# A router that reads the output projection's transposed result, with x kept transposed

## What is computed

```python
h = jnp.einsum('btd,de->bte', x, w_in)                 # 2048 -> 4352
...                                                    # conv, chunk MLP, pooling give y (2048 wide)
mix = jnp.einsum('bte,ed->btd', y, w_out)              # 2048 -> 2048
x = layer_norm(ALPHA * x + mix, ln1_g, ln1_b)
g_logits = (xt @ rg_w).astype(jnp.float32) + rg_b      # 4 expert groups, top 1
e_logits = ((xt @ re_w).astype(jnp.float32) + re_b)    # 16 experts, top 2 within the group
hg = jnp.einsum('nd,edf->nef', xt, w_gate)             # 2048 -> 512 for each of 16 experts
hu = jnp.einsum('nd,edf->nef', xt, w_up)
a = jax.nn.silu(hg) * hu * combine[:, :, None]
out = jnp.einsum('nef,efd->nd', a, w_down)
x = layer_norm(ALPHA * x + out, ln2_g, ln2_b)
```

## Time and profile before

| | us |
|---|---|
| median of 3 runs (lowest, highest) | 895.5 (894.67, 897.81) |
| the profiled execution, its own time | 897.55 |
| its span | 895.7 |
| PE busy | 838.7 |
| DVE, ACT, POOL busy | 282.4, 263.8, 24.8 |
| mixer, to the last chunk's end | about 0 to 394 |
| router, to the first expert matmul | about 394 to 427 |
| experts and the last LayerNorm | about 427 to 896 |

### The profile page before, as it was taken

One profiled execution on the slowest core, in us unless ns is written; L12 is line 12 of the kernel. 1 busy time (PEld: TensorE's weight loads), 2 busy tenths in 40 slices (PEclk: granted clock), 3 DMA queues, 4 the chain that ended last, 5 costly groups with the idle time before them and its releaser, 6 DMA issues.

```text
span 895.7 us, 11202 instructions
## 1 busy us (share of the span) xinstructions
PE 838.7 (94%) x4729; PEld 558.7 (62%) x4729; DVE 282.4 (32%) x390; ACT 263.8 (29%) x465; POOL 24.8 (3%) x41
## 2 busy tenths in 40 slices
PE   6999999999999999995989999999999998897993
PEld 6989999999999999983433334433333333333331
DVE  6273384434764435355000102043003220022203
ACT  5234232322233323312432332432223322133101
POOL 0000000000001000001000000000000100000000
PEclk8999999999999999996899999999999999999997
DMA  9643553665444774459898999999999999999980
GB/s 298 185 142 120 188 164 127 192 205 164 144 140 153 282 282 141 141 220 384 353 426 351 421 423 422 428 418 423 424 425 420 424 426 420 422 424 425 421 355 37
DMA packets 81149, 267.80 MB, mean 299 GB/s; under 512 B 5626, under 2 KB 58320, under 8 KB 59657
## 3 DMA queue, kind: packets, MB, share of 16 engines
q1 hardware_dynamic: 78042, 258.92, 74.6%
q0 software_dynamic: 1984, 5.31, 1.5%
q10 hardware_dynamic: 1078, 2.94, 1.0%
HBM read 263.07 MB, written 11.54 MB: 307 GB/s over the span
## 4 chain that ended last, share of the span: by engine, by line
PE 68%; DMA 18%; DVE 6%; ACT 3%; SPq 2%; issue 2%; POOL 0%; POOLq 0%; ACTq 0%; DVEq 0%
PE ps L1284 16%; PE ps L476 12%; PE ps L477 12%; PE ps L478 12%; DMA gu_w<-in_expert_w_up 7%; PE ps L1318 6%; DMA down_w<-in_expert_w_down 4%; DMA xg<-z_rows,row 3%; PE ps L1220 3%; DMA out<-xg,sample_row 3%; SPq L398 2%; ACT xT L1390 1%; PE ps L529 1%; DVE xg L1639 1%; PE ps L1261 1%
## 5 line engine op out<-in xcount | busy, mean ns | idle before, releaser
L1284 PE MATMUL ps<-gu_w,xT 128*64 128x512 f32 x1024 | 235.3, 601 | 14.7 <-DMA gu_w<-in_expert_w_up 13.7
L657 DVE TENSOR_TENSOR w_lo<-raw,w_hi 128x2048 fp32r<-128x2048 f32 x50 | 114.5, 2291 | 173.5 <-ACT w_hi L649 171.9
L1284 PEld LDWEIGHTS ps<-gu_w,xT 128*64 128x64 f32 x1024 | 72.6, 138 | 142.5 <-issue 136.4
L476 PE MATMUL ps<-xT_hi,w_hi 128*128 128x320 f32 x512 | 159.2, 311 | 0.0
L477 PE MATMUL ps<-xT_lo,w_hi 128*128 128x320 f32 x512 | 158.3, 309 | 0.0
L478 PE MATMUL ps<-xT_hi,w_lo 128*128 128x320 f32 x512 | 158.2, 309 | 0.0
L649 ACT ACTIVATE w_hi<-raw 128x2048 fp32r<-128x2048 f32 x49 | 93.8, 1915 | 210.0 <-DMA raw<-in_w_in 138.1
L1390 ACT ACTIVATE xT<-ps,gbT 128x64 f32<-128x64 f32 x256 | 82.2, 406 | 158.7 <-PE ps L1220 158.7
L1318 PE MATMUL ps<-down_w,aT 128*64 128x512 f32 x480 | 106.5, 596 | 0.6
L1661 DVE TENSOR_TENSOR a_sb<-ps,a_sb 128x256 f32<-128x256 f32 x16 | 6.8, 424 | 289.4 <-ACT a_sb L1444 289.4
L476 PEld LDWEIGHTS ps<-xT_hi,w_hi 128*128 128x128 f32 x512 | 96.1, 188 | 0.5
(11 more groups left out here) (261 smaller groups left out, 523.4 us busy)
## 6 DMA issues: line engine op xcount, KB each, us to landing
gu_w<-in_expert_w_gate SPq DMA_DIRECT2D x64, 1024.0 KB, 15.3
gu_w<-in_expert_w_up SPq DMA_DIRECT2D x64, 1024.0 KB, 19.0
down_w<-in_expert_w_down SPq DMA_DIRECT2D x32, 2048.0 KB, 24.1
raw<-in_w_in SPq DMA_DIRECT2D x34, 1024.0 KB, 5.3
raw<-in_w_out SPq DMA_DIRECT2D x16, 1024.0 KB, 5.4
tok<-in_x_prompt SPq DMA_DIRECT2D x2, 1024.0 KB, 6.0
z_rows<-tok ACTq DMA_DIRECT2D x2, 768.0 KB, 4.1
tok<-in_x_sample SPq DMA_DIRECT2D x1, 512.0 KB, 9.1
```

The costliest lines, as they stand in the source:

```text
L476: pe.matmul(out, wh[:, t, col], hi[:, kt, :], start=(n == 0 and t == 0), stop=False)
L657: dve.tensor_tensor(w_lo[k][:, :], raw[k][:, :], w_hi[k][:, :].bitcast(FP32), ALU.subtract)\
L1284: last = pe.matmul(ps[C * side:C * (side + 1), GU, :], x, w[:, :, c, FH * side:FH * (side + 1)], start=(j == 0 and c == 0), stop=(j == PAI ...
```

## The change

The change makes the sum ALPHA*x + y @ w_out in the transposed layout. x is kept as `x_all`, which POOL puts together from `xT_hi` and `xT_lo` in four additions, and `tok` is given up after the first transposes. DVE makes `zt` from PSUM and `x_all` (`make_zt`), PE multiplies `zt` by the router's weights between the chunks of the next group (`route`) and turns it to rows (`rows_of`), ACT copies the rows to `z_part` and stores them group by group (`copy_rows`, `store_rows`), and DVE takes the statistics there (`row_sums`). Only the last four of the router's 16 feature tiles are left for after the last chunk, whose products are made column by column. x and w_in are read as (t p) in place of (p t), and the router's weights and LayerNorm's vectors too; these loads move from ACT's and POOL's queues at chunk 34 to SP's queue behind chunk 8. `raw[s]` and `w_hi[s]` lie side by side and make one 16 KB slot each. Units 5 and 6 are issued about two chunks before the mixer's end, unit 7 one chunk before it, units 8 and 9 at the end, unit 10 after the logits and the second `xg`'s zeroing as before. Two half units move from w_out's chunks to chunks 28 and 32.

```diff
-    raw = [at(f"raw{s}", RAW0 + s * 8 * KB, [P, CH]) for s in range(3)]
-    slot_at = [EARLY0, EARLY0 + 16 * KB, T0 + 32 * KB, T0, T0 + 16 * KB, RAW0 + 16 * KB, RAW0 + 32 * KB,
-               YT_HI0 + 22 * KB, TOK0, RAW0, XA + 24 * KB]
+    raw = [at(f"raw{s}", RAW0 + s * 16 * KB, [P, CH]) for s in range(3)]
...
+    w_hi = [at(f"w_hi{s}", RAW0 + 8 * KB + s * 16 * KB, [P, CH], F32R) for s in range(RING)]
+    w_lo = [at(f"w_lo{s}", RAW0 + s * 16 * KB, [P, CH], F32R) for s in range(RING)]
...
+    x_all = at("x_all", XA, [P, KT, NTOK])
+    zt = [at(f"zt{s}", LATE + s * 2 * ROW, [P, 2, NTOK]) for s in range(3)]
+    z_part = [at("z_part0", XA + 4 * XT_B, [P, 3, GW]), at("z_part1", XA + XT_B, [P, 3, GW])]
...
-    win_v = w_in[0].rearrange("(p t) n -> p t n", t=KT)
+    win_v = w_in[0].rearrange("(t p) n -> p t n", p=P)
...
+            if c == 8:
+                sp.wait_ge(x_full, 12)
+                sp.dma_start(rg_nat[:, :, :], rg_w[0].rearrange("(t p) n -> p t n", p=P)).then_inc(rw_in, 16)
+                sp.dma_start(re_nat[:, :, :], re_w[0].rearrange("(t p) n -> p t n", p=P)).then_inc(rw_in, 16)
+                for k, src in enumerate((ln1_g, ln1_b)):
+                    sp.dma_start(gb_nat[:, k, :], src[0].rearrange("(t p) -> p t", p=P),
+                                 allow_slow_non_contiguous=True).then_inc(gb_nat_in, 16)
+            if c in (12, 16, 20, 24, 28, 32):
...
+            if n and by_column:
+                for f in range(2):
+                    out, col = ps[:, 2 * pair + f, 0:NTOK], slice(P * f, P * (f + 1))
+                    for t in range(CK):
+                        kt = CK * halves[n] + t
+                        pe.matmul(out, wh[:, t, col], hi[:, kt, :], start=False, stop=False)
+                        pe.matmul(out, wh[:, t, col], lo[:, kt, :], start=False, stop=False)
+                        last = pe.matmul(out, wl[:, t, col], hi[:, kt, :], start=False, stop=(t == CK - 1))
+                    last.then_inc(w_used if f else first_column, 1)
...
+        def route(tiles):
+            for kt in tiles:
+                j = kt % RQ
+                last = pe.matmul(ps[RP * j:RP * (j + 1), LGB, 0:NTOK], rw[:, kt, :], zt[kt // 2 % 3][:, kt % 2, :],
+                                 start=(kt < RQ), stop=(kt >= KT - RQ))
+            return last
...
+        def rows_of(k, columns):
...
+            for f in columns:
+                pe.wait_ge(zt_ready, k + 1 + (f if k == 7 else 0))
+                if f == 0:
+                    if k == 0:
+                        wait_read(pe, "z0", "z1")
+                    else:
+                        pe.wait_ge(rows_read, 3 * k)
+                for i in range(2):
+                    pe.transpose(ps[:, ROWB, GW * i + P * f:GW * i + P * (f + 1)],
+                                 zt[k % 3][:, f, P * i:P * (i + 1)], ident[:, :])
+                out, samples_of = ps[64 * f:64 * (f + 1), 2 * ((G_O + k) % 3), NTOK:NTOK + P], zt[k % 3][:, f, SEQ:NTOK]
+                if f == 0:
+                    last = pe.transpose(out, samples_of, ident[:, :])
+                else:
+                    last = pe.matmul(out, samples_of, ident[:, :], start=True, stop=True)
+            return last
...
+        def behind(k):
+            def step(n):
+                if n != CK - 1:
+                    return
+                rows_of(k, (0, 1)).then_inc(rows_made, 1)
+                if k % 2:
+                    if k == 1:
+                        pe.wait_ge(rw_ready, 4)
+                    route(range(2 * k - 2, 2 * k + 2)).then_inc(zt_used, 1)
+                if k == 6:
+                    pe.wait_ge(sums_ready, 2)
...
-        with pe.Fori(0, 2) as s:
-            for i in range(3):
-                group_products(pe, G_O + 1 + i, Y, HALF_O, s, 3)
-                out_tokens(i, s)
-        group_products(pe, G_END - 1, Y, HALF_O)
-        out_tokens(6)
-        out_tokens(7)
+        for k in range(1, 8):
+            group_products(pe, G_O + k, Y, HALF_O, between=behind(k - 1), by_column=(k == 7),
+                           free=(zt_ready, k - 2) if k >= 3 else None)
+        rows_of(7, (0,))
+        route(range(KT - 4, KT - 1))
+        rows_of(7, (1,)).then_inc(rows_made, 1)
+        route(range(KT - 1, KT)).then_inc(lgT_made, 1)
...
+    def copy_rows(act, k):
+        act.wait_ge(rows_made, k + 1)
...
+        part = z_part[k % 2]
+        act.activation(part[:, 0:2, :], ps[:, ROWB, :].rearrange("p (i c) -> p i c", i=2), ACT.Copy).then_inc(rows_read, 1)
+        for f in range(2):
+            act.activation(part[0:64, 2, P * f:P * (f + 1)], ps[64 * f:64 * (f + 1), 2 * ((G_O + k) % 3), NTOK:NTOK + P],
+                           ACT.Copy).then_inc(rows_read, 1)
+    def store_rows(act, k):
+        act.wait_ge(rows_read, 3 * (k + 1))
+        col, part = slice(GW * k, GW * (k + 1)), z_part[k % 2]
+        act.dma_start(z_dram[0:SEQ, col].rearrange("(i p) c -> p i c", p=P), part[:, 0:2, :]).then_inc(z_stored[k % 2], 16)
+        act.dma_start(z_dram[SEQ:NTOK, col], part[0:64, 2, :]).then_inc(z_stored[k % 2], 16)
...
+        for k in range(6):
+            split_hi(act, 2 * (G_O + k) + 4)
+            copy_rows(act, k)
+            store_rows(act, k)
+            if k == 0:
+                act.wait_ge(x_whole, 4)
+                act.dma_start(rbias[:, 0:NG], rg_b[0:1, :]).then_inc(rbias_in, 16)
+                act.dma_start(rbias[:, NG:NG + NE], re_b[0:1, :]).then_inc(rbias_in, 16)
+            split_hi(act, 2 * (G_O + k) + 5)
+        copy_rows(act, 6)
+        store_rows(act, 6)
+        copy_rows(act, 7)
...
+        def make_zt(k, columns=slice(0, 2)):
+            pair = (G_O + k) % 3
+            if k == 0:
+                dve.wait_ge(x_whole, 4)
+            if k >= 3:
+                dve.wait_ge(zt_used, (k - 3) // 2 + 1)
+            a, b = columns.start, columns.stop
+            last = dve.scalar_tensor_tensor(out=zt[k % 3][:, columns, :], in0=x_all[:, 2 * k + a:2 * k + b, :],
+                                            scalar=ALPHA, in1=ps[:, 2 * pair + a:2 * pair + b, 0:NTOK],
+                                            op0=ALU.mult, op1=ALU.add)
+            last.then_inc(zt_ready, 1)
+        def row_sums(k):
+            part = z_part[k % 2]
+            dve.wait_ge(rows_read, 3 * k + 1)
+            for i in range(2):
+                steps.inc(dve.bn_stats(xstats[:, i, k, :], part[:, i, :]))
+            dve.wait_ge(rows_read, 3 * k + 3)
+            dve.bn_stats(xstats[0:64, 2, k, :], part[0:64, 2, :]).then_inc(rows_seen, 1)
+        for k in range(8):
+            c = 2 * (G_O + k) + 2
+            if c < CHUNKS1:
+                split_lo(dve, c)
+            if k:
+                row_sums(k - 1)
+            if k < 7:
+                dve.wait_ge(w_used, c)
+                make_zt(k)
+            else:
+                dve.wait_ge(first_column, 1)
+                make_zt(7, slice(0, 1))
+                dve.wait_ge(w_used, CHUNKS1)
+                make_zt(7, slice(1, 2))
+            if c + 1 < CHUNKS1:
+                split_lo(dve, c + 1)
+            if k == 0:
+                router_weights()
+        row_sums(7)
+        dve.wait_ge(rows_seen, 8)
...
-        sp.wait_ge(w_used, CHUNKS1)
-        order = [EARLY, EARLY + 1, SLOTS, EARLY + 2, SLOTS + 1, SLOTS - 1] + list(range(FIRST, len(ORDER)))
-        for i in order:
+        for i in range(EARLY, len(ORDER)):
             e, u = ORDER[i]
             s = slot(i)
-            if i == SLOTS:
-                store_z(sp, 8, slice(6 * GW, 8 * GW))
-            if i == SLOTS - 1:
-                sp.wait_ge(z_stored, 16 * 6)
-                sp.wait_ge(zT_full, 12)
-            if i == SLOTS + 1:
+            if i == EARLY:
+                sp.wait_ge(w_used, CHUNKS1 - 2)
+            elif i == EARLY + 1:
+                sp.wait_ge(zt_ready, 7)
+            elif i == EARLY + 2:
+                sp.wait_ge(w_used, CHUNKS1 - 1)
+            elif i == EARLY + 3:
+                sp.wait_ge(w_used, CHUNKS1)
+            elif i == FIRST - 1:
...
+        pool.wait_ge(w_used, 2 * G_O)
+        for q in range(4):
+            four = slice(4 * q, 4 * q + 4)
+            pool.tensor_tensor(x_all[:, four, :], xT_hi[:, four, :].bitcast(FP32), xT_lo[:, four, :].bitcast(FP32),
+                               ALU.add).then_inc(x_whole, 1)
...
         pool.wait_ge(w_used, CHUNKS1)
-        pool.memset(lgT[:, NTOK:3 * P], 0.0).then_inc(lgT_pad, 1)
+        pool.wait_ge(rows_seen, 7)
+        pool.wait_ge(z_stored[0], 32 * 4)
         pool.memset(xg[0][:, :], 0.0).then_inc(xg_zero, 1)
-        pool.wait_ge(z_stored, 16 * 6)
-        pool.wait_ge(zT_full, 12)
+        pool.wait_ge(rows_seen, 8)
+        pool.wait_ge(z_stored[1], 32 * 4)
...
-        turn_z(0)
-        turn_z(1)
-        pe.wait_ge(rw_ready, 4)
-        route(0)
-        turn_z(2)
-        route(1)
-        turn_z(3)
-        route(2)
...
+        act.wait_ge(lgT_made, 1)
```

(4 more changed lines are left out.)

252 lines of the change are left out of this document (82 added, 170 removed).

## The result

The changed kernel takes 901.35 us (median of 7 runs, 899.5 to 902.29), the kernel before 896.52 us in the runs beside it. The ratio is 1.0052, 95% interval 1.0039 to 1.0064. So it is slower by 0.5%, where 889.5 us was forecast, and lies outside the range of 885.5 to 895. The profiled execution took 902.29 us.

The account below looks back on a forecast made before the run. The first expert's start was taken to set the weight stream and thereby the end. Logits gain 9.45 less PE's 4.1, plus 0.9 from the gather, made 6.25, taken as 6.0: 895.5 - 6.0 = 889.5 us, range 885.5 to 895.

Parts of the forecast that it names:

- Part 6: Mixer, from about 276 us: POOL's additions run beside DVE's `w_lo` and `yT_lo` and cost nothing.
- The sign of being wrong: Near 280 us: `w_lo` or `yT_lo` starting late or running long would show the forecast wrong.
- The rival: Near 280 us: POOL and DVE exclude each other, delaying DVE 2.7 to 8.7 us; 892.2 to 898.2, likeliest 893; chance 0.21.
- Part 2: Mixer: PE, already full, takes over `route`, bias matmuls and row transposes; loss 4.1 us.
- Part 1: Handover: logits start 5.6 us after the reaction to the last chunk, before 15.3; gain 9.45 us after two copies.
- Part 4: Gather and first expert: token numbers 5.35 us earlier, gather 2 us shorter, 0.9 of it counting; gain taken 6.0 us.
- The last store holds the gather: Handover: a store taking 12 us makes the gather 4 late, less 0.9 of DVE's cover; 892.6 us; chance 0.11.
- Part 5: Early mixer: four strided loads, 8192 pieces, cost 4.1 to 23.8 us; low end taken, hidden up to 13.7 us.
- Part 3: Mixer: DVE's and ACT's added work costs nothing, each addition being below 4.7 us of slack before PE waits.
- What bounds the kernel: Whole kernel: the first expert's start sets the weight stream, which sets the end; starting x earlier shortens it by about x.

## Why the prediction was wrong

**The step that failed: Part 6, POOL's additions at nothing.** It was seen that they run just while the chain goes through DVE, and the case was put among the rivals at 0.21. Undone, it gives back 6.3 us by the medians; alone, it costs 4.2. In the traces it is a wait of 4.50 in place of 0.89 us and then 2.2 us at the lower clock, 5.8 together. The sign of being wrong that the prediction named for this (`w_lo` or `yT_lo` running long near 280 us) is what came. The rival had the mechanism and the size right: an addition takes 2.96 us alone where 2.9 was given for two inputs, and its cost of 2.7 to 8.7 us holds the 5.8. It did not have the clock, and its low end of 2.7 cannot be worked out from its own figures (three halves of 1.44 us are 2.2). Its range, 892.2 to 898.2, ended 3 us below the time, because Parts 2 and 4 failed as well. That a row was missing for the wait was taken as evidence against it; POOL had simply not worked there.

**Part 2, mis-sized.** Forecast a loss of 4.1 us on PE. The set of rows was priced as before (0.65) with 0.1 more for the ordinary product. It costs 1.10: seven sets less six of before are 7 x 1.10 - 6 x 0.65 = 3.8 in place of 1.35. With `route` (2.0) and the bias (0.65) it is 6.45. With the product turned into a transpose 2.25 us came back by the medians, 2.5 in the traces, about the excess of 2.35.

**Part 1, nearly right.** Forecast R + 5.6 for the logits, measured R' + 7.1. Of the 1.5, 0.85 is `vstd` under the zero fill. That the handover gets shorter by turning the rows inside the mixer was right: the token numbers were to gain 9.45 us and gained 8.05 (R + 19.87 before, R' + 11.82 after).

**Part 4, half.** The gather was to be issued at R + 11 and to be 2 us shorter. It went out at R' + 15.6 and did take less, 5.8 us where it was 8.5. It waited for the last store, issued at 406.79 and 407.19 and landed 10.1 and 11.5 us after. The rival "The last store holds the gather" had this right (12 us, the gather 4 late); the 3.1 us of the whole time that it put on it are not shown, for without this wait the median falls by 0.8. On DVE's side `facts` waited 2.4 us, for the gather's issue and the fill behind it. In sum the first expert gained 6.9 over the handover, where 10.1 were forecast. But experiments that took away each hindrance, or both, gained nothing measurable. For the store the reason is shown: what it gains by landing early, the gather loses beside the weights. What the 3.2 us are worth to the whole time stays open.

**Part 5, right.** The four strided loads were hidden. SP issued them from 59.94 to 66.93 us, the longest in 3.94 us. The windows of 66 to 74 us, before and after:

```profile
66.00:74.00 8.00, 7.89 (x54) 7.17 (x53) 4.65 (x4) 3.31 (x5) 0.00 (x0) 1.00 0.21 57
```

```profile
66.00:74.00 8.00, 8.00 (x56) 8.00 (x55) 3.10 (x3) 3.09 (x4) 0.00 (x0) 1.00 0.54 44
```

They add to the DMA share and hardly to the GB/s. The page counts 13849 packets under 512 B, 5626 before, about the 8192 pieces more. PE is busy throughout these windows, and chunk 9 is rounded at 77.44 (79.97 before, the lead of 2.5 kept). Over 58 to 82 us the share rose from 0.41 to 0.61: 0.2 x 24 = 4.8 us of all engines, near the 4.1 that was taken.

**Part 3 held.** With the additions on DVE itself, PE still waits only 0.21 us.

**What bounds the kernel**, right: from the first expert's start to the end it is 470.2 us before (897.55 - 427.33) and between 469.6 and 472.5 in the profiles of the change and of its variants. The end follows the first expert, with a scatter of up to 2 us that no run here explains; the change's profile has 472.3.

**The account.** Against the kernel before, -6.0 us were forecast and +4.85 measured (901.35 - 896.5), 10.85 more. The profiled execution can be followed step by step: 891.55 was forecast for it and 902.29 measured, 10.7 more. The additions are 5.8 of this, the rows of z and what else Part 2 missed 2.3, the handover 3.2, and 2.1 came behind the first expert. The lead of 2.8 from the start, which was the luck of that one execution, goes off. That makes 10.6. By medians the additions are 6.3, and with 2.35 and 3.2 the sum is 11.85 for 10.85; the medians can't check it more closely.
